# Six pairs of gate blocks as half-depth products, and the residual transposed inside the output projection

## The reference

```
u = rms_norm(x)
z = u @ w_in                      # latents, rope key, retention q/k/v/gate, 2 x 1024 gate columns
y_a = MLA(z) @ w_proj_mla
y_r = (silu(rg) * head_norm(retention(z))) @ w_proj_ret
g_a, g_r = split(sigmoid(gates + b_gate))
h = x + (g_a * y_a + g_r * y_r) @ w_out
```

## Time and profile before

| | before |
|---|---|
| median of three runs | 1805.42 us |
| span of the profiled execution (first to last instruction) | 1807.1 us |
| TensorE busy | 1759.0 us, 97% |
| VectorE, ScalarE, GpSimd busy | 60%, 39%, 54% |
| from the fifth gate block to the latents | 342.5 to 524.1 us |
| granted TensorE clock, mean | 0.993 of full |

### The profile page before, as it was taken

One profiled execution on the slowest core, in us unless ns is written; L12 is line 12 of the kernel. 1 busy time (PEld: TensorE's weight loads), 2 busy tenths in 40 slices (PEclk: granted clock), 3 DMA queues, 4 the chain that ended last, 5 costly groups with the idle time before them and its releaser, 6 DMA issues.

```text
span 1807.1 us, 25034 instructions
## 1 busy us (share of the span) xinstructions
PE 1759.0 (97%) x8599; PEld 1467.8 (81%) x8599; DVE 1087.8 (60%) x1535; ACT 698.0 (39%) x1243; POOL 982.2 (54%) x554
## 2 busy tenths in 40 slices
PE   7999999999999899999999999999999999999998
PEld 7888888888888677788878888778888888878887
DVE  5655663002334778884345564887777777889842
ACT  7422223111013667731133232644444444444432
POOL 6743333445654577654433232577777777655540
PEclk9999999999999999999999999999999999999999
DMA  6511111347661789583221134243433334494322
GB/s 266 204 52 36 36 43 49 139 164 256 227 227 46 276 317 325 177 308 113 103 71 59 59 104 141 77 139 107 142 117 123 133 110 139 142 344 143 122 76 93
DMA packets 111245, 262.33 MB, mean 145 GB/s; under 512 B 7744, under 2 KB 50368, under 8 KB 106688
## 3 DMA queue, kind: packets, MB, share of 16 engines
q1 hardware_dynamic: 84720, 182.13, 30.3%
q10 hardware_dynamic: 26448, 79.18, 11.8%
HBM read 186.82 MB, written 73.92 MB: 144 GB/s over the span
## 4 chain that ended last, share of the span: by engine, by line
PE 84%; DVE 6%; ACT 5%; issue 2%; DMA 1%; POOL 1%; ACTq 0%; DVEq 0%; SPq 0%; POOLq 0%
PE ps L714 16%; PE ps L719 16%; PE ps L720 16%; PE ps L1333 7%; PE ps L1338 7%; PE ps L1335 7%; PE ps L1408 2%; PE ps L1409 2%; PE ps L1410 2%; ACT prow L1792 2%; PE ps L1110 1%; PE ps L1090 1%; DMA raw<-in_slabs 1%; DVE aneg L2570 1%; PE ps L1431 1%
## 5 line engine op out<-in xcount | busy, mean ns | idle before, releaser
L609 POOL TENSOR_SCALAR wh<-raw 128x1024 fp32r<-128x1024 f32 x75 | 211.6, 2822 | 467.3 <-PE ps L714 448.9
L714 PE MATMUL ps<-uh,wh 128*128 128x512 f32 x560 | 221.2, 395 | 0.7 <-POOL wl L602 0.7
L720 PE MATMUL ps<-uh,wl 128*128 128x512 f32 x560 | 218.4, 390 | 0.0
L719 PE MATMUL ps<-ul,wh 128*128 128x512 f32 x560 | 218.0, 389 | 0.0
L611 POOL TENSOR_TENSOR wl<-raw,wh 128x1024 fp32r<-128x1024 f32 x75 | 182.0, 2427 | 6.3
L646 POOL TENSOR_TENSOR wl<-raw,wh 128x512 fp32r<-128x512 f32 x88 | 137.5, 1573 | 69.1 <-ACT wh L1457 67.8
L633 POOL TENSOR_TENSOR over_rings<-over_rings 128x512 f32<-128x512 f32 x92 | 118.2, 1285 | 51.5 <-DMA over_rings<-in_slabs 45.9
L1457 ACT ACTIVATE wh<-raw 128x512 fp32r<-128x512 f32 (+1 forms) x164 | 105.4, 656 | 88.9 <-PE ps L1338 58.0
L689 POOL TENSOR_TENSOR wl<-raw,wh 128x512 fp32r<-128x512 f32 x63 | 93.7, 1496 | 78.2 <-ACT wh L1457 78.2
L2212 DVE SCALAR_TENSOR_TENSOR ya<-zA,sm,ya 128x512 f32<-128x512 f32 x88 | 109.6, 1246 | 31.7 <-ACT ya L2036 24.6
L720 PEld LDWEIGHTS ps<-uh,wl 128*128 128x128 f32 x560 | 105.1, 188 | 22.6
(11 more groups left out here) (488 smaller groups left out, 4873.9 us busy)
## 6 DMA issues: line engine op xcount, KB each, us to landing
raw<-in_slabs SPq DMA_DIRECT2D x110, 512.0 KB, 3.6
over_rings<-in_slabs SPq DMA_DIRECT2D x22, 1024.0 KB, 7.1
s_s<-over_rings SPq DMA_DIRECT2D x22, 1024.0 KB, 4.9
ssm<-s_s SPq DMA_DIRECT2D x22, 512.0 KB, 4.5
raw<-s_s SPq DMA_DIRECT2D x22, 512.0 KB, 3.8
s_f<-yb ACTq DMA_DIRECT2D x22, 512.0 KB, 5.3
raw<-s_d SPq DMA_DIRECT2D x36, 256.0 KB, 2.5
dsum<-in_slabs SPq DMA_DIRECT2D x16, 512.0 KB, 6.7
```

The source lines that it names most:

```text
L609: pool.tensor_scalar(wh[:, j, :], raw[:, j % RAWS, :], 1.0, None, ALU.mult).then_inc(S["w_hi"], 1)
L714: l = pe.matmul(o, lh, rh, start=start, stop=False)
L719: pe.matmul(o, lh, rl, start=False, stop=False)
L720: return pe.matmul(o, ll, rh, start=False, stop=stop)
```

## The change

- "ga" keeps four dense gate blocks. The retention's projection ("pr", four slabs of two blocks) comes right behind them; ScalarE copies its blocks to `yrs` and stores them to a new `s_yr`.
- The other twelve gate blocks are six pairs (`GP = 6`), each seven products of 4 k x 3 matmuls (`gate_pair`). VectorE makes the sums of u ahead of them (`turns`, four quarters of 8 sums and 4 low parts), the sums of the weights (`gate_sum`: S1, S3, S2, S4), and the outputs out of the products (`quarter`: u2, u4, c22, c12, c21). ScalarE makes the high parts of the seven weights and the sigmoids, GpSimd the low parts. The last four pairs are multiplied by the retained y (`gate_times`), which ScalarE loads back.
- The down sums have one tile `dsum_gates` for the first six, so that a load waits for the store before it. SyncE issues store and load ahead of the two slabs of a pair. Two more of the sums have tiles of their own and come behind the latents' slabs.
- `x_turn`, `xtile`, `xst` and `s_x` are gone. In the mixture x's columns are loaded as they are (128 x 8 pieces of 512 bytes per block) into `hT`, and TensorE transposes them onto the banks of the output projection before its matmuls accumulate there (`residual`); VectorE then copies instead of adding.

SyncE's order and its waits:

```diff
+            def gate_slab(i, r):
+                if i == 0:
+                    sp.wait_ge(S["w_ready"], SLAB0["gp"] + r - RAWS + 1)
+                elif r == 0:
+                    sp.wait_ge(S["gp_lo"], glo(i - 1, VS4))
+                else:
+                    sp.wait_ge(S["w_ready"], SLAB0["gp"] + 2 * i)
+                sp.dma_start(raw[:, r, :], slabs[gate_at(GD + 2 * i + r)]).then_inc(S[f"ld{r}"], 16)
             def down_load(p):
-                if p >= 4:
-                    sp.wait_ge(S[f"ld_k{p % 4}"], 16 + 48)
-                down_rows_in(p, dsum[p % 4], f"ld_k{p % 4}")
+                if p == 0:
+                    sp.wait_ge(S["gt_lo"], GB + 4 * CH)
+                else:
+                    sp.wait_ge(S["ds_ld"], 16 + 48 * p)
+                down_rows_in(p, dsum_gates, "x_ld1")
...
+            for i in range(GP):
+                if i >= 2:
+                    if i > 2:
+                        down_store(i - 3)
+                    down_load(i - 2)
+                for r in range(RAWS):
+                    gate_slab(i, r)
+            for n in range(2):
+                down_store(GP - 3 + n)
+                down_load(GP - 2 + n)
+                slab(SLAB0["lat"] + 2 * n)
+                slab(SLAB0["lat"] + 2 * n + 1)
```

TensorE, a pair (the first one has another order and waits for u's sums):

```diff
+                gate_product(i, VA11, q, u_at(0, 0))
+                gate_product(i, VS2, q + 1, t_at("t2"))
...
+                gate_product(i, VS1, q + 2, t_at("t1"))
+                gate_product(i, VS3, q + 3, t_at("t3"))
+                pe.wait_ge(S["gp_act"], ga_at(i, "p1c"))
+                gate_product(i, VA12, q, u_at(CH, 0), True)
+                pe.wait_ge(S["gp_v"], gv_at(i, "u4"))
+                gate_product(i, VS4, q + 2, u_at(CH, 1), True)
+                pe.wait_ge(S["gp_v"], gv_at(i, "c22"))
+                gate_product(i, VA22, q + 3, t_at("t4"), True)
```

VectorE, a turn (S1 waits for both slabs of the next pair, S2 and S4 for the low parts of its A11 and A12):

```diff
+            for i in range(GP):
+                more = i + 1 < GP
+                if i:
+                    quarter(i - 1, "c21")
+                quarter(i, "u2")
+                if i > 2:
+                    gate_times(i - 1, "B0")
+                if more:
+                    gate_sum(i + 1, VS1)
+                    gate_sum(i + 1, VS3)
+                quarter(i, "u4")
+                if more:
+                    gate_sum(i + 1, VS2)
+                quarter(i, "c22")
+                if i >= 2:
+                    gate_times(i, "B1")
+                    gate_times(i, "A0")
+                if more:
+                    gate_sum(i + 1, VS4)
+                quarter(i, "c12")
+                if i >= 2:
+                    gate_times(i, "A1")
+                if i >= 1:
+                    down_sums(i - 1)
```

TensorE, the output projection:

```diff
+            def residual(m):
+
+                def rows_in(b):
+                    for j in range(CH):
+                        c = slice((CH * b + j) * P, (CH * b + j + 1) * P)
+                        pe.matmul(ps[:, b, j * P:(j + 1) * P], hT[:, m, c], ident, start=j == 0, stop=False,
+                                  is_transpose=True, skip_group_check=True)
+                return rows_in
+            pe.wait_ge(S["x_ld0"], 16 + 16 * KB)
```

More of the change, by code:

```diff
@@ L80 @@
 RAWS = 2
+GD = 4
+GP = (2 * KB - GD) // 2
+GSKIP = 4
 PI = 3.1415925
@@ L595, in _, with split @@
         def _(pool):
-            def split(i, j, made=0, both=True):
+            def split(i, j, made=0, both=True, skipped=0):
                 s = SLOTS * i + j
@@ L916, in _ @@
                 dense(j, SLAB0["ga"] + j, USE0["ga"] + j, KB, of(uh, ul), between=pair)
[L917 to L920, removed]
             pe.wait_ge(S["y_lo"], 2 * RH)
[L925 to L932, removed]
-                        dense(j, s, u, RH, of(yth, ytl), between=between)
@@ new lines, in _ @@
+            turn_hi(1, "t3")
+            gate_hi(0, VA11)
+            retained(4)
+            turn_hi(1, "t2")
+            retained(5)
+            turn_hi(1, "t4")
+            retained(6)
+            gate_hi(0, VS2)
+            retained(7)
+            act.wait_ge(S["fin_st"], 16 * MB + 16)
+            turn_hi(2, "t1")
+            retained(8)
+            gate_hi(0, VS1)
+            gate_hi(0, VS3)
+            retained(9)
+            turn_hi(2, "t3")
+            retained(10)
+            turn_hi(2, "t2")
@@ L1704, in _ @@
+            sigmoid(GP - 1, "sB0")
+            gate_store(GP - 1, "A1")
+            gate_store(GP - 1, "B0")
+            for name in ("zA0", "zA1", "zB0", "zB1"):
+                act.wait_ge(*gz_store(name, GP))
             for j in range(4):
@@ new lines, in quarter @@
+            def quarter(i, name):
+                q = 4 * (i % 2)
+                v, o, p_, bank, op, after = {
+                    "u2": (VS2, gu2[:, :], gu4, q + 1, ALU.add, None),
+                    "u4": (VS1, gu4[:, :], gu2, q + 2, ALU.subtract, "u2"),
+                    "c22": (VS3, gzB[:, half(1)], gu4, q + 3, ALU.add, "u4"),
+                    "c12": (VS4, gzA[:, half(1)], gu2 if i else gu4, q + 2 if i else 6, ALU.subtract, "u4"),
+                    "c21": (VA22, gzB[:, half(0)], gu2, q + 3, ALU.add, "u2")}[name]
+                dve.wait_ge(S["gp_done"], gdone(i, v))
+                if name == "u2":
+                    dve.wait_ge(S["gp_act"], ga_at(i, "p1c"))
+                    if i:
+                        dve.wait_ge(S["gp_v"], gv_at(i - 1, "c21"))
+                if after:
+                    dve.wait_ge(S["gp_v"], gv_at(i, after))
+                if i and name[0] == "c":
+                    dve.wait_ge(*gz_store({"c22": "zB1", "c12": "zA1", "c21": "zB0"}[name], i))
+                dve.tensor_tensor(o, p_[:, :], ps[:, bank, :], op).then_inc(S["gp_v"], 1)
@@ L2467, in _ @@
-            for i in range(KB // 2):
-                mul_r(i, i == 0)
-            dve.wait_ge(S["g_st0"], 16 * KB)
-            dve.wait_ge(S["g_st1"], 16 * KB)
-            for q in range(2):
-                dve.wait_ge(S[f"ld_k{q}"], PAIR_LD)
+            turns(0)
+            turns(1)
+            gate_sum(0, VS1)
+            gate_sum(0, VS3)
+            gate_sum(0, VS2)
+            turns(2)
+            gate_sum(0, VS4)
+            for b in range(2):
+                dve.wait_ge(d_done[b], USE0["pr"] + KB)
```

507 lines of the change are left out of this document (364 added, 143 removed).

## The result

The change makes the kernel slower: 1843.51 us (median of 4 runs, 1840.12 to 1846.30) against 1804.99 for the kernel before beside it (4 runs, 1803.38 to 1806.05). The ratio is 1.0211, 95% interval 1.0194 to 1.0227. The forecast was 1830, slower. Measured is +38.5 us where the sum said +25.1; 1843.5 lies inside the stated range (1807 to 1846), near its upper end.

What follows compares the result with a forecast made beforehand. TensorE, busy 97% of the span, was taken as the bound, with a ring through SyncE's order stalling it after the change: -16.3 - 6.7 + 7.5 + 39.2 + 1.4 = +25.1 us, forecast 1830 us, range 1807 to 1846.

Steps and rivals of the forecast that it cites:

- The ring: From pair 3, down sum, store, loads and VectorE's S1 wait in a circle: 30.0 us a turn against 19.04; 76 in 100.
- the prediction's clock: Times in the pairs' stage counted from 0 at the first pair, put at 386.9 us of the trace.
- stall: TensorE idle in the pairs and before the latents: +39.2 us, 8 to 10 in each of four places, 0.9 in pair 0.
- cold clock: Ahead of the latents, idle TensorE then runs seven matmuls at half clock: +1.4 us; in the pairs hidden by the ring's slack.
- the late quarter of u's sums: Before the first pair, VectorE's last quarter of u sums starts when the projection ends, late by at most 1 us.
- Three terms in the ring: Slab landing to end of down sums 16.3 us, store 5.0 with two waits, loads to the next slab 8.7.
- x's columns: Ahead of the output projection, the last x loads land up to 6.8 us after being asked for: at most 1 us late.
- The transposes: x's 64 transposes come back in front of the output projection's halves: 6.7 us and eight more switches of 0.1, +7.5 us.
- The work taken off: In the gate stage, 72 fewer matmuls over six pairs, -16.3 us, and x's transposes leaving, -6.7 us.
- rival (a): The ring doesn't bind and the change gives what it takes off: -12.5 us, 1793; 13 in 100.
- rival (b): VectorE itself bounds the pairs through collisions with GpSimd: 21 us a pair, 12 us over six, 1805; 5 in 100.
- Rival (c): The sums of u are late too, colliding with the split of projection slab 4: +7 us on the forecast, 1837; 6 in 100.

Runs made afterwards that it cites:

- Experiment 1: The changed kernel with SyncE asking for the gate slabs and the latents' first slabs ahead of the down sums' store and loads: 1808.56 us, ratio 1.0026.
- Experiment 9: The changed kernel with each down sum made of 8 columns instead of 512, store and loads whole: 1834.15 us, ratio 1.0167.
- experiment 2: The changed kernel with SyncE's order as store, then slabs, then down rows, in the pairs and before the latents: 1828.47 us, ratio 1.0136.
- experiment 4: The changed kernel with x's loads one by one behind the mixture's copies, waited for in two halves: 1836.07 us, ratio 1.0179.
- experiments 6 and 8: 6: the changed kernel with the edits of Experiment 1 and experiment 4, 1801.17 us; 8: 6 without the residual's transposes, x added as it lies, 1793.81 us.
- experiment 7: The changed kernel with slabs first, x's loads behind the mixture's copies, and the pairs' last down sums behind the last product: 1796.59 us, ratio 0.9952.
- experiment 10: The kernel of experiment 7 with each down sum made of 8 columns instead of 512: 1791.71 us, ratio 0.9932.

## Why the prediction was right in its sign and short in its size

**The ring: right.** Its links were forecast as 16.3 + 5.0 + 8.7 = 30.0 us and measured as 16.9 + 3.9 + 9.3 = 30.1; the turn after took 31.4, with an S1 at 505.82. On the prediction's clock the slabs' landings were due at 446.1, 476.1 and 506.1. S1, which waits for them, came at 444.35, 474.41 and 505.82. The last down sum before the latents was due at 522.4 and ended at 522.8, and the latents' slab was due out of GpSimd at 540.4, which was 542.3. Experiment 1 takes the ring out and moves the token sums by 38.9 us, with a new wait of 3.0 in it; 40.6 had been counted for stall and cold clock. Experiment 9 shortens one link by 2.1 us, and the same turn follows by 2.1; experiment 2 takes the loads out, and the turn is the sum of the links that remain. The "about 1 us" for the late quarter of u's sums held: from 387 to 407 us TensorE is busy for 19.2 of 20.

**Three terms in the ring were off and cancelled.** The store landed 1.1 us sooner than 5.0, the loads and slabs took 0.6 longer, the way to the down sum 0.6. That the sum is within 0.1 us is luck. From the Trainium skill, "SBUF — State Buffer", The DMA setup-cost knee, came the estimates of 4.4 us for the store and 6.8 for the four loads. The trace has 3.8 to 4.0 and 9.3, so the Trainium skill's line is above the one, and well below this burst on one queue.

**Cold clock: mis-sized, and read at the wrong place.** The term was 1.4 us, from seven matmuls said to stand behind a short wait. There is no wait: the list of TensorE's waits in the kernel before is empty from 540 to 570 us. What stands ahead of them are the token sums, 32 matmuls of two columns each:

```profile
560.39 1.84 PE L952 MATMUL ps<-cn,lz 128*128 128x2 f32 x16
562.10 1.93 PE L952 MATMUL ps<-cn,lsq 128*128 128x2 f32 x16
563.88 0.43 PE L961 MATMUL ps<-uh,wh 128*64 128x512 f32 x1
```

The same stretch of half clock follows the token sums in the kernel after (585.6 to 588.6 us), so it is no part of the difference. What a true wait costs behind it shows at the latents: after 6.7 us idle the clock over the first 18 us was 0.84, and from the latents' first matmul to the token sums it is 2.6 us more than before.

**x's columns: the step that failed.** The prediction priced x's loads by their landing ("at most 1 us") and put their issues at nothing; its "about 0.34 us each" was for those of the pairs. But these loads are cut into 1024 pieces of 512 bytes and two of them stood right behind twelve others: they held ScalarE's queue for 8.26 us, which moved the mixture, and the last load with it. The landing was priced well (5.65 us). It is the issue, expected 7.1 us before TensorE wants the columns (810.93 and 818.0), that came 0.2 us behind (840.38 and 840.16). The wait (5.9) and the matmuls at half clock behind it make up what experiment 4 gets back, 7.4 us by the medians, 7.7 by the marks. Of the 12.3 us by which the traces exceed the sum this is the largest part. The pieces stood in the change's own text, and the down rows' loads, cut the same way, show an issue of 2.22 us at 433.45; I looked at the landing and not at the engine that must issue them. That 1843.5 still lies inside the range is in part luck: its upper end was room for a slower store and slower loads in the ring, and x's columns used it.

**The transposes: right.** 7.5 forecast, 7.4 measured (experiments 6 and 8). Between their two traces it is 9.3 (361.0 and 351.7 us from the token sums to those behind the output projection), so this part is good to some 2 us only.

**The work taken off: right in its stage, less over the whole kernel.** In the stage it was -16.3 - 6.7 = -23.0. Without the ring the latents start at 502.7 (experiment 1) and 503.1 (experiment 7) instead of 524.1: -21.4 and -21.0, with 1.6 and 2.0 us of small waits in it. For the whole kernel the sum without stall was -15.5, and -12.5 as rival (a) with its own small waits. Experiment 7 comes to -9.6 by the medians and -8.7 by the ratio, 3 to 4 short of (a), and no run shows where these went. The spans of the two profiled executions, 1792.4 and 1807.1, are 14.7 apart, but the one was among its kernel's fastest, and the other was longer than any of the three timed runs beside it. Rival (a) was thus, to within some 4 us, what the change could have done, and not what this order let it do. Of rival (b) little is left: it asked for 12 us over six pairs, and in experiment 7 TensorE idles for 2.0 us of 163, and for 0.8 with VectorE's work thinned (experiment 10). Rival (c) showed nowhere: the wait for u's last sums was 0.8 us.

## What to carry to other kernels

A queue written out by hand is part of the dependency graph. Where a store that waits for an engine's last work of a turn stands ahead of the loads for the same engine's first work of the next, the turn is as long as their sum, however idle each is; walk it once round and compare with the work of the busiest engine. Ask of each moved load who issues it, in how many pieces and behind what, not only when it lands. And put transfers that nobody waits for soon (here the down rows) behind those that are waited for: the same work went from 2.1% slower to 0.5% faster by order alone.

## What the runs showed of the hardware that I had not expected

- Two loads in 512-byte pieces (1024 pieces, 512 KB each) took 8.26 us to issue on ScalarE's queue right behind twelve other loads, ahead of a plain copy; with rows of 4 KB the two took 0.99 us. Spread between the mixture's copies (experiment 4), loads in the same pieces took 0.39 to 2.17 us each.
- Two slabs of 512 KB asked for 0.4 us behind a 1 MB store on the same queue were usable 9.2 us later; the median slab takes 3.6 us.
- After an idle time of 7.43 us TensorE ran 11 matmuls at 0.43 us each before it was back at 0.23.
- TensorE's clock fell without any wait, in the stretch of 32 matmuls of two columns each and behind it: to 0.68 from 540 to 545 us in experiment 7, and to 0.66 from 564 to 569 us in the kernel before. In the trace of experiment 10 the same 32 matmuls ran from 537.4 us on and the clock stayed at 1.00 up to 561. Why it fell in the one and not in the other stays open.
